# Order of the transposes within one attention step: the sampled quad's turns ahead of the prompt's turns

## What is computed

```
proj = rmsnorm(x) @ w_in                   # queries, 3 sets of keys/values, gates, convolution inputs
# each branch: s = q k^T * 64^-0.5 - slope * distance;  p = softmax(s);  o = p v
o = g0 * o_compressed + g1 * o_selected + g2 * o_window        # sparse attention, 8 heads of 64
conv = swish(layernorm(depthwise_conv31(a * sigmoid(b))))
x = x + concat(o, conv) @ w_out
x = x + square(relu(rmsnorm(x) @ w_up)) @ w_down               # hidden width 4096
x = x + (p @ w_ple) * sigmoid(rmsnorm(x) @ w_ple_gate)
y = rmsnorm(x)
```

## Time and profile before

| | us |
|---|---|
| median of 3 runs (2009.77 to 2020.17) | 2019.97 |
| the profiled execution's own time | 2015.92 |
| its span | 2014.3 |
| TensorE busy, share of the span | 1878.7, 93% |
| VectorE, ScalarE, GpSimd busy | 902.2, 647.8, 593.7 |
| attention steps, first prompt turn to last | 622.6 to 968.6 |
| mean granted TensorE clock, share of full | 0.966 |

### The profile page before, as it was taken

The page is one execution under the profiler, slowest core; times in us unless marked ns, Lnnn a source line. Parts: engine busy times, 40 slices in busy tenths (PEclk is TensorE's granted clock), DMA queues, the critical chain, the costliest instruction groups (busy, mean ns, idle before and its releaser), DMA issues. The chain is left out here.

```text
span 2014.3 us, 35248 instructions
## 1 busy us (share of the span) xinstructions
PE 1878.7 (93%) x13394; PEld 1748.5 (87%) x13394; DVE 902.2 (45%) x1589; ACT 647.8 (32%) x1203; POOL 593.7 (29%) x610
## 2 busy tenths in 40 slices
PE   7999989898997999999798999999999999998897
PEld 6999988787995666666697999999999999998897
DVE  4699945555546676766423121212121221225322
ACT  4311223233334665666332221111212121213233
POOL 0004862212404444344252222222221212224231
PEclk8999978998998999999898999999999999998998
DMA  4321364433613343342413111111111202011112
GB/s 152 95 76 43 89 189 134 108 84 85 161 51 106 102 124 119 106 133 73 135 46 123 48 32 53 37 53 45 40 53 37 60 28 66 27 48 58 37 42 86
DMA packets 188229, 160.41 MB, mean 80 GB/s; under 512 B 23108, under 2 KB 171281, under 8 KB 187423
## 3 DMA queue, kind: packets, MB, share of 16 engines
q1 hardware_dynamic: 170445, 133.87, 22.6%
q0 software_dynamic: 6336, 17.31, 3.3%
q10 hardware_dynamic: 11290, 7.09, 1.3%
HBM read 144.55 MB, written 18.25 MB: 81 GB/s over the span
## 5 line engine op out<-in xcount | busy, mean ns | idle before, releaser
L202 POOL TENSOR_TENSOR wm_lo<-wm_raw,wm_hi 128x512 fp32r<-128x512 f32 (+1 forms) x96 | 169.0, 1761 | 563.0 <-ACT wm_hi L197 563.0
L2272 DVE TENSOR_TENSOR xT<-ps_m,xT 128x1056 f32<-128x1056 f32 x64 | 80.5, 1258 | 260.0 <-PE ps_m L216 260.0
L1476 POOL TENSOR_SCALAR S<-S,inv,gate_p 128x64 f32<-128x64 f32 (+6 forms) x192 | 122.7, 656 | 196.6 <-DVE inv L1778 196.6
L216 PE MATMUL ps_m<-Ahi,wm_hi 128*128 128x352 f32 x768 | 167.2, 326 | 2.1 <-issue 2.1
L216 PE MATMUL ps_m<-Hhi,wm_hi 128*128 128x352 f32 x768 | 166.7, 325 | 1.3 <-POOL wm_lo L202 1.3
L912 PE MATMUL ps_p<-Xhi,w1hi 128*128 128x256 f32 (+1 forms) x544 | 164.8, 303 | 2.8 <-DVE Xlo L1096 2.8
L216 PE MATMUL ps_m<-Alo,wm_hi 128*128 128x352 f32 x768 | 165.7, 324 | 0.0
L216 PE MATMUL ps_m<-Ahi,wm_lo 128*128 128x352 f32 x768 | 165.5, 323 | 0.0
L216 PE MATMUL ps_m<-Hhi,wm_lo 128*128 128x352 f32 x768 | 165.5, 323 | 0.0
L197 ACT ACTIVATE wm_hi<-wm_raw 128x512 fp32r<-128x512 f32 (+1 forms) x96 | 73.8, 769 | 284.9 <-PE ps_m L216 284.9
L216 PE MATMUL ps_m<-Hlo,wm_hi 128*128 128x352 f32 x768 | 165.3, 323 | 0.0
(11 more groups left out here) (366 smaller groups left out, 3928.7 us busy)
## 6 DMA issues: line engine op xcount, KB each, us to landing
s_raw<-in_cache_slc_kv_dram SPq DMA_DIRECT2D x256, 128.0 KB, 2.1
raw<-in_cache_cmp_kv_dram SPq DMA_DIRECT2D x128, 128.0 KB, 4.1
raw<-in_cache_cmp_kv_dram POOLq DMA_DIRECT2D x128, 128.0 KB, 4.5
wm_raw<-in_w_up_dram SPq DMA_DIRECT2D x32, 512.0 KB, 4.1
wm_raw<-in_w_down_dram SPq DMA_DIRECT2D x64, 256.0 KB, 2.8
win_raw<-in_w_in_dram SPq DMA_DIRECT2D x38, 256.0 KB, 3.4
xT<-x_spill SPq DMA_DIRECT2D x2, 2112.0 KB, 7.9
x_rows<-in_x_prompt_dram SPq DMA_DIRECT2D x8, 512.0 KB, 5.5
```

The lines of the kernel that those rows point to most:

```text
L202: self.c.nc.gpsimd.tensor_tensor(self.lo[s][:, 0:nk, :], self.raw[s % self.raw_slots][:, 0:nk, :], self.hi[s][:, 0:nk, :].bitcast(F32), AL ...
L216: mm = nc.tensor.matmul(ps[:, j, 0:CH], w[s][:, k, :], x(k)[:, CH * j:CH * j + CH], start=(k == 0 and n == 0), stop=(k == nk - 1 and n == 2))
L1476: nc.gpsimd.tensor_scalar(x, x, inv[:, n % 3, 3 * e + br:3 * e + br + 1], c.gate_p[:, i, H * br + h:H * br + h + 1], ALU.mult, ALU.mult).t ...
L2272: nc.vector.tensor_tensor(three(x), ps[s][:, :, 0:CH], three(x), ALU.add).then_inc(W.free, 1)
```

## The change

In each step that has them, the second key half and the weights turn now come before the prompt's one or two turns. The same is done in the list `TURNS`, on TensorE, in ScalarE's copies and in VectorE's copy of the last key bank. (VectorE's copies of the odd prompt groups already stood behind its sums of a quad.) Nothing is added or removed, and no instruction of GpSimd or of the DMA queue on SyncE moves.

```diff
     for st in range(NS):
         n = unit_of_step[st]
-        TURNS += [("p", k) for k in steps[st]]
         z = quad_at(st, 1)
         TURNS += [("k", z, bb) for bb in (2, 3) if z is not None]
         z = weighed_at(st)
         if z is not None:
             TURNS += [("q", z)] + [("n", z)] * (place(z) < 2)
+        TURNS += [("p", k) for k in steps[st]]
...
                     st = first_step[n] + j
-                    for k in steps[st]:
-                        turn(k)
                     z = quad_at(st, 1)
                     if z is not None:
                         turn_keys(z, 1)
                     z = weighed_at(st)
                     if z is not None:
                         turn_weights(z)
+                    for k in steps[st]:
+                        turn(k)
                     for ch in share:
                         qk(n + 2, ch)
...
-                    for k in steps[st]:
-                        if k % 2 == 0:
-                            keep(k)
                     z = quad_at(st, 1)
                     if z is not None:
                         keep_keys(z, 2)
                     z = weighed_at(st)
                     if z is not None:
                         keep_weights(z)
+                    for k in steps[st]:
+                        if k % 2 == 0:
+                            keep(k)
...
                     z = quad_at(st, 3)
                     if z is not None:
                         quad_sums(z)
+                    z = quad_at(st, 1)
+                    if z is not None:
+                        keep_keys(z, 3)
                     for k in steps[st]:
                         if k % 2 == 1:
                             keep(k)
-                    z = quad_at(st, 1)
-                    if z is not None:
-                        keep_keys(z, 3)
```

## The result

The change makes the kernel slower by 0.43% (ratio 1.0043, 95% interval 1.0034 to 1.0053, 19 runs of each): a median of 2025.30 us against 2015.51 us. Two of the three runs of before that the prediction had seen lay high; over 19 runs its median is 4.5 us lower, and close to the 2015.92 us of the profiled execution. The ratio, which goes by the averages and not by the medians, means 8.7 us; its interval goes from 6.9 to 10.7.

A forecast was written before the change was run, and what follows sets the result against it. TensorE's program order bounds the attention steps, with 22.5 us of holes. Terms 4.3 + 2.3 + 0.1 - 1.1 = 5.6 us on 2015.92 give 2021.5, predicted as 2022 us, range 2011 to 2033.

The forecast's parts named there:

- the sum: All terms together, 4.3 + 2.3 + 0.1 - 1.1 = 5.6 us slower, on the profiled execution's 2015.92 us.
- Part 1, the five late steps: Weights turns already waiting for ScalarE's exponentials each lose 0.86 us of prompt turns that covered the wait: 4.3 us slower.
- The light steps: Ten weights turns that don't wait today: 1.7 us lost, plus 0.6 us for quads 1 and 10's second banks; 2.3 us.
- Quads 0, 17, 9: Three special weights-turn steps: 0.7 us lost behind late VectorE work, 0.4 net cover lost, 1.0 gained on a bank wait.
- Part 2, the key halves: Second key halves going first hide prompt turns' waits for GpSimd in steps 5 (0.8 us) and 27 (0.3 us): minus 1.1 us.
- Part 3, the followers: ScalarE's and VectorE's copies, output bank emptying, SyncE's refill and GpSimd's distances: the new order costs them nothing.
- the old fall: Clock drop in the kernel before, granted 0.85, 0.50, 0.80 over three 2 us stretches; priced at 1.7 us of clock time.
- The signs: If right: exponentials' wait 8 or 10 us in 12 or more, GpSimd waits down 1 to 2, steps 5 to 6 longer.
- One sign of being wrong: Within the stretch from first to last prompt turn, the clock shows several stretches at 0.50.
- The faster one: Rival: freer banks shorten output bank waits and late exponentials move forward; up to 3.5 + 2 us gained, 2010.5 us; chance 0.09.
- The null one: Rival: late steps' delay is given back at the next wait for GpSimd; 2016 to 2018 us; chance 0.13.
- The clock rival: Longer TensorE holes lower its clock: five falls of 1.7 us add 8.5 us, 2030 us, 0.7% slower; chance 0.13.

The follow-up runs named there:

- the filled kernel: The change plus 14 identity transposes before the wait for the exponentials in the five late steps; ratio to the kernel before 1.0033, 6.6 us slower.
- the two kernels that split the change: Against the kernel before: only the 18 weights turns moved ahead of the prompt turns, ratio 1.0056; only the 18 second key halves moved ahead, ratio 0.9991.

## Why the prediction was right, point by point

The sign, the place and the mechanism of lost cover held. The size was 8.7 us where the sum said 5.6 (3.1 short), inside the range: the sum had the cover right and no share for the clock. The predicted 2022 us lies 3.3 us under the median of 2025.30. To take the profiled execution as the base rather than the median of three was the right choice.

**Part 1, the five late steps (4.3 us).** Right. In both traces I took the starts of the same turns and saw how their distance grew over each step. Around the weights turns of quads 3, 7 and 16, where the clock stayed full in both, it grew by 0.88, 0.85 and 0.87 us: the 0.86 of lost cover. Around quads 2 and 4 it grew by 3.7 and 3.4 us, since the clock fell there.

**The light steps (2.3 us).** 2.3 us by the same reading. Quad 1 lost 0.7 and quad 10 lost 0.5, where 0.47 was costed for each; quads 5, 14 and 15 lost nothing and the other five 0.2 or 0.3 each.

**Quads 0, 17, 9 (+0.7, +0.4, -1.0).** +0.7, +0.4 and -1.2.

**Part 2, the key halves (-1.1 us).** -1.2 us in all, but by other steps than I thought, so part of that agreement is luck. The two steps gave 0.8 and 0.3 us as costed. Steps 41 and 63 lost 0.44 us each, where `pv` waits 0.94 instead of 0.41 us for the output bank. The small holes of other steps gave back some 0.4 us, and step 69, behind quad 14's key half, 0.6 us. "GpSimd's other waits lie in steps that hold no key half" is true of step 69, but its wait depends on the step before. There VectorE's copy of the last key bank no longer comes behind the step's last turn, and the inverse and GpSimd's scaling follow that copy. The scaling starts at 901.11 before and at 911.61 in the change, 10.5 us later, when `pv` beside it starts 11.15 us later (900.64 and 911.79). That the key half is the cause is shown by the two kernels that split the change; the path over VectorE's copy is read from the traces and was not run by itself.

**Part 3, the followers (nothing).** The waits for the output bank grew by 1.5 us (8.6 against 7.1), and 0.9 us of time went there, in steps 41 and 63. "Stands behind all copies of its step in both orders" is true, but which copy ScalarE does last had changed: with the even prompt group as the fourth turn, the bank is emptied 0.5 us later.

**The sum** without the clock is by these readings 4.3 + 2.3 + (0.7 + 0.4 - 1.2) - 1.2 = 5.3 us, and 5.6 us by the filled kernel. It was right within 0.3 us.

**The clock.** This is the term that was missing from the forecast and stood in a rival at 0.13. I priced a fall at 1.7 us, asked for five of them and gave them no share in the sum. In the profiled execution there were two new ones of about 2.7 us each. The mistake was to treat the falls as all or nothing: two of five, the case that came, had no place in it, though the prediction had said itself that the change makes holes of just the size that preceded the old fall. The Trainium skill's page "TensorE: Matmul & The Clock Gate", section "A second HAM failure mode: psum-queue depth-cycling", tells of a kernel that cycled through its PSUM banks and whose short idle stretches between groups of matmuls made the clock swing. The trace bears out that such idle stretches can bring the clock down (0.59 in 8 us around a hole of 2.08 us), but not that the cycle does it: the three-bank cycle is in every kernel here, and with the holes filled the clock is 1.00 over 331 us of it.

**The signs.** The 1.05 us wait in quad 9's step is gone, and the stages outside the steps stayed within 0.5 us, as said. The weights turn's wait for the exponentials went past what was named (12.1 us in 11 waits, not 8 or 10 in 12 or more), and so did the fall of the waits for GpSimd (2.9 us, not 1 to 2; about 1.1 of it vanished into quad 4's hole) and the length of the steps (10.7 us, not 5 to 6). One sign of being wrong came true: the clock showed several stretches at 0.50. The output bank's waits changed by less than the 2 us named.

**The rivals.** The faster one is excluded. The null one is not seen: no late step's delay was given back at a wait for GpSimd. The clock rival came true in part, with two falls of the five that it asked for.

## What to carry to other kernels

A wait at the head of an in-order queue costs its whole length; the same wait behind ready work costs only what the ready work doesn't cover. So put the turn whose input is latest last, or make its producer's queue bring it sooner: here a wait behind 0.86 us of ready work grew dearer by 0.85 to 0.88 us when that work was put behind it. Moving a quad's exponentials and the emptying of a bank in ScalarE's program gave more (ratio 0.9978) than any order of TensorE's turns tried without it (0.9991 at best). When an edit lengthens TensorE's idle stretches, add a share for the clock to the forecast instead of leaving it to a rival: price a fall from the trace, count the long new holes, and let some of them bring one. Here it was two of five, three of five and two of five in three executions. And look at which copy each engine does last in a step: in this change that alone moved an output bank by 0.5 us one way and GpSimd's start by 0.6 us the other.

## What the runs showed of the hardware that I had not expected

The length of a hole alone doesn't tell whether the clock falls. In the change holes of 2.08 and 2.69 us (quads 2 and 4) led to 1.2 GHz, while quad 7's, of the same cause, left no window under 1.00 from 740 to 824; with the weights turns alone quads 4 and 7 had falls and quad 2 none. A fall can also be dearer than the one I had priced: stretches of 8 us at 0.59 and 0.57 in the change, against 6 us at 0.72 before; the two with the weights turns alone cost as much clock time as the old one. And idle time can be filled at no loss: 70 transposes that nobody reads made the steps 6.4 us shorter in the profiled executions, and the granted clock of the timed runs rose from 0.9643 to 0.9667; in the times the gain (ratio 1.0033 against 1.0043) is within the intervals.
